# Six gate chunks of the second wide projection moved from one dense stage into three attention stages

## What is computed

```python
u = rmsnorm(x, norm_mix[l]) * (1.0 + scale1) + shift1
aq, ak, av, bq, bkv, biq, bik, biw, cq, ck, cv, g = split_cols(u @ w_in[l])
y_a = diff_attention(aq, ak, av, ...) @ w_br_a[l]
y_b = dsa_attention(bq, rmsnorm(bkv, dsa_kv_norm[l]), biq, bik, biw, ...) @ w_br_b[l]
y_c = moba_attention(cq, ck, cv, bias_c) @ w_br_c[l]
gates = jax.nn.sigmoid(g + gate_b[l]).reshape(B, S, 3, D_MODEL)
merged = gates[:, :, 0] * y_a + gates[:, :, 1] * y_b + gates[:, :, 2] * y_c
x = x + gate1 * (merged @ w_o[l])
```

## Time and profile before

| | us |
|---|---|
| median of three runs | 1955.89 |
| lowest and highest run | 1954.1, 1958.25 |
| span of the profiled execution | 1951.6 |
| PE busy in it | 1747.7 (90%) |
| DVE busy | 1018.7 (52%) |
| ACT busy | 826.7 (42%) |

### The profile page before, as it was taken

One profiled execution on the slowest core, in us unless ns is written; L12 is line 12 of the kernel. 1 busy time (PEld: TensorE's weight loads), 2 busy tenths in 40 slices (PEclk: granted clock), 3 DMA queues, 4 the chain that ended last, 5 costly groups with the idle time before them and its releaser, 6 DMA issues.

```text
span 1951.6 us, 22498 instructions
## 1 busy us (share of the span) xinstructions
PE 1747.7 (90%) x8447; PEld 1421.4 (73%) x8447; DVE 1018.7 (52%) x1239; ACT 826.7 (42%) x979; POOL 75.6 (4%) x122
## 2 busy tenths in 40 slices
PE   6999968799989999899899888999889896779996
PEld 6788857688868888798655576888677783558885
DVE  4545555454454545455666454545457653555444
ACT  4555523365543434334433333655334443314342
POOL 0000000000000000000000001000010010000000
PEclk9999989999989999999656798999989986789999
DMA  8565633566554556525344536655545520345550
GB/s 286 168 191 185 214 119 97 194 194 189 180 180 152 168 187 193 172 82 167 106 141 123 201 103 206 216 181 192 173 175 175 170 91 11 133 158 193 192 174 22
DMA packets 197807, 314.82 MB, mean 161 GB/s; under 512 B 16185, under 2 KB 120661, under 8 KB 197232
## 3 DMA queue, kind: packets, MB, share of 16 engines
q1 hardware_dynamic: 191824, 288.90, 45.1%
q0 software_dynamic: 5920, 25.06, 3.6%
HBM read 309.71 MB, written 4.21 MB: 161 GB/s over the span
## 4 chain that ended last, share of the span: by engine, by line
PE 85%; DVE 7%; ACT 2%; issue 2%; POOL 1%; PEld 1%; DVEq 1%; DMA 0%; PEldq 0%; ACTq 0%; POOLq 0%
PE ps L1865 24%; PE ps L1867 23%; PE ps L1866 23%; PE ps L2143 2%; PE ps L1911 2%; PE ps L2128 1%; DVE wlo L1218 1%; PE ps L1952 1%; PE ps L2037 1%; PE ps L2119 1%; DVE gain L1266 1%; PE ps L2139 1%; DVE xn L1288 1%; PE ps L2191 1%; ACT xn L778 1%
## 5 line engine op out<-in xcount | busy, mean ns | idle before, releaser
L1218 DVE TENSOR_TENSOR wlo<-raw,whi 128x2048 fp32r<-128x2048 f32 x255 | 579.0, 2290 | 305.1 <-ACT whi L722 304.4
L722 ACT ACTIVATE whi<-raw 128x2048 fp32r<-128x2048 f32 x255 | 481.2, 1910 | 177.6 <-PE ps L1867 163.2
L1865 PE MATMUL ps<-wlo,aT_hi 128*128 128x512 f32 (+1 forms) x1280 | 499.9, 391 | 18.9 <-issue 8.3
L1867 PE MATMUL ps<-whi,aT_hi 128*128 128x512 f32 (+1 forms) x1280 | 493.3, 385 | 0.0
L1866 PE MATMUL ps<-whi,aT_lo 128*128 128x512 f32 (+1 forms) x1280 | 493.1, 385 | 0.0
L1865 PEld LDWEIGHTS ps<-wlo,aT_hi 128*128 128x128 f32 x1280 | 243.9, 191 | 68.5 <-issue 10.5
L1867 PEld LDWEIGHTS ps<-whi,aT_hi 128*128 128x128 f32 x1280 | 243.2, 190 | 48.1
L1866 PEld LDWEIGHTS ps<-whi,aT_lo 128*128 128x128 f32 x1280 | 244.0, 191 | 45.2
L1865 PE MATMUL ps<-wlo,hT_hi 128*128 128x512 f32 x480 | 187.2, 390 | 8.4 <-DVE hT_lo L1327 6.0
L1867 PE MATMUL ps<-whi,hT_hi 128*128 128x512 f32 x480 | 187.0, 389 | 0.0
L1866 PE MATMUL ps<-whi,hT_lo 128*128 128x512 f32 x480 | 186.8, 389 | 0.0
(11 more groups left out here) (274 smaller groups left out, 1445.8 us busy)
## 6 DMA issues: line engine op xcount, KB each, us to landing
raw<-in_ffn_w_in SPq DMA_DIRECT2D x176, 512.0 KB, 4.8
raw<-in_ffn_w_out SPq DMA_DIRECT2D x88, 512.0 KB, 4.3
raw<-in_w_ff SPq DMA_DIRECT2D x64, 512.0 KB, 4.8
raw<-in_ada_w SPq DMA_DIRECT2D x48, 512.0 KB, 4.7
raw<-in_w_in SPq DMA_DIRECT2D x48, 512.0 KB, 4.6
raw<-in_xattn_w_kv SPq DMA_DIRECT2D x32, 512.0 KB, 6.7
raw<-in_xattn_w_q SPq DMA_DIRECT2D x16, 512.0 KB, 5.4
raw<-in_xattn_w_o SPq DMA_DIRECT2D x16, 512.0 KB, 6.3
```

Source lines behind the costliest of these rows:

```text
L722: act.activation(to, of, ACT.Copy).then_inc(hi_ready[slot], 1)
L1218: dve.tensor_tensor(lo, of, hi, ALU.subtract).then_inc(lo_ready[slot], 1)
L1865: pe.matmul(o, lh, rl, start=start, stop=False, skip_group_check=True)
L1867: return pe.matmul(o, lh, rh, start=False, stop=stop, skip_group_check=True)
```

## The change

Only the index chunk, `aq`, `ak` and `av` stay in `wide_inputs`. Each attention stage now runs two of the gate chunks on PE, whole, ahead of the transposes of units 0 and 4, when the scores of units 1 and 5 (2 and 6 in `moba`) are already queued. `gate_part` writes them to two PSUM banks of one half of the tokens each, and DVE's `keep_gate` adds them to the bias later. To free those banks, `diff` holds two units of scores instead of three. The splits of the gate slabs, and of the chunks that follow a stage, stand between the units in ACT's and DVE's queues. The two `dsa` stages are one of eight units. The sigmoids move to `merge`, three of 128 x 2048 in place of six of 128 x 1024. The choice of keys for tokens 128 to 255 runs all eight rounds in one piece in `wide_inputs`; that for tokens 0 to 127 is in `sparse_inputs`.

```diff
                 def wide_inputs(self):
...
-                    chunk(w, COLS["g"], 512, 0)
...
-                    for c in range(1, 6):
-                        chunk(w, COLS["g"] + 512 * c, 512, 2 * ((c + 1) % 2))
...
+                def diff(self):
+                    stages.next()
+                    self.gate(0)
+                    self.gate(1)
...
+        def gate_place(c):
+            return 2 * ((0, 1, 1, 0, 1, 0)[c]), (6, 7) if c < 4 else (3, 7)
```

PE, the new helper and its call in `diff` (`dsa` and `moba` call it with chunks 2, 3 and 4, 5):

```diff
+                def gate_part(self, c, q):
+                    (pair, banks), t, s = gate_place(c), q // 2, q % 2
+                    if c and s == 0:
+                        pe.wait_ge(gate_kept, 2 * c + t - 1)
+                    if t == 0:
+                        pe.wait_ge(lo_ready[pair + s], uses.next(pair + s))
+                    tok = slice(t * P, (t + 1) * P)
+                    for r in range(4):
+                        k = 4 * s + r
+                        last = parts(ps[:, banks[t], :], aT_hi[:, k, tok], aT_lo[:, k, tok], ...
...
-                    score(1)
                     for u in range(8):
-                        if u + 2 < 8:
-                            score(u + 2)
-                        self.turn_probs(u, u % 2, 6, depth=3, banks=1)
+                        if u + 1 < 8:
+                            score(u + 1)
+                        if u % 4 == 0:
+                            for q in range(4):
+                                self.gate_part(u // 4, q)
+                        self.turn_probs(u, u % 2, 4, depth=3, banks=1)
                         if u:
                             values(u - 1)
```

ACT in `diff` (in `dsa` and `moba` two splits stand likewise after units 0 and 1, and two after units 5, 6 or 6, 7):

```diff
                     exps(0)
-                    exps(1)
                     for u in range(8):
+                        if u + 1 < 8:
+                            exps(u + 1)
                         keep(u)
-                        if u + 2 < 8:
-                            exps(u + 2)
                         if u:
                             out(u - 1)
+                        if u < 2:
+                            split(2 + u)
+                        if u == 4:
+                            self.gate_used(0)
+                        if u > 5:
+                            split(u - 6)
```

DVE in `diff`:

```diff
                     top(0)
-                    top(1)
                     for u in range(8):
+                        if u + 1 < 8:
+                            top(u + 1)
                         weigh(u)
-                        if u + 2 < 8:
-                            top(u + 2)
+                        if u < 2:
+                            split(2 + u)
+                        if u in (2, 4):
+                            self.keep_gate(0, u // 2 - 1)
+                        if u == 6:
+                            self.keep_gate(1, 0)
+                        if u > 5:
+                            split(u - 6)
+                    self.keep_gate(1, 1)
```

More of the change, by code:

```diff
@@ L445, in skip, with gate, dsa @@
                     stages.next()
-                ada = diff_bias = diff = latent = dsa = skip
+                ada = diff_bias = latent = skip
+                def gate(self, c):
+                    chunk(A["w_in_2"][0], COLS["g"] + 512 * c, 512, gate_place(c)[0])
+                def diff(self):
+                    stages.next()
+                    self.gate(0)
+                    self.gate(1)
+                def dsa(self):
+                    stages.next()
+                    self.gate(2)
+                    self.gate(3)
                 def moba(self):
                     stages.next(2)
+                    self.gate(4)
+                    self.gate(5)
                 def wide_inputs(self):
@@ L1011, in rectify, with gate_used @@
                                     act.activation(o, o, ACT.Relu).then_inc(relu_made, 1)
-                    chunks(10, evac, transfers=[(1, 6)], after=rectify)
+                    chunks(4, evac, after=rectify)
                     leave()
+                def gate_used(self, c):
+                    for s in range(2):
+                        done.next(gate_place(c)[0] + s)
                 def keep_bias(self, b):
@@ new lines, in dsa @@
+                    exps(0)
+                    for u in range(8):
+                        if u + 1 < 8:
+                            exps(u + 1)
+                        keep(u)
+                        if u == 4:
+                            latent_out(0)
+                        if u == 5:
+                            out(0)
+                        if u < 2:
+                            split(u)
+                        if u == 4:
+                            self.gate_used(2)
+                        if u in (5, 6):
+                            split(u - 3)
@@ L1112, in dsa @@
+                    latent_out(1)
+                    out(1)
+                    self.gate_used(3)
+                    units.next(8)
+                    groups.next(2)
                     leave()
@@ new lines, in wide_inputs, with choose_keys, keep_gate @@
+                    chunks(4, evac, after=choose)
+                    leave()
+                def choose_keys(self, t):
+                    step(dve.tensor_scalar(sel[t], work[t].rearrange("p (k n) -> p k n", n=P), -2.0e38, NEG,
+                                           ALU.is_gt, ALU.mult))
+                def keep_gate(self, c, t):
+                    pair, banks = gate_place(c)
+                    if c == 0:
+                        dve.wait_ge(gate_b_in, 32)
+                    dve.wait_ge(gate_summed, 2 * c + t + 1)
+                    at = bgate[:, t, 512 * c:512 * c + 512]
+                    dve.tensor_tensor(at, at, ps[:, banks[t], :], ALU.add).then_inc(gate_kept, 1)
+                    if t:
+                        for s in range(2):
+                            done.next(pair + s)
@@ L2311, in dsa @@
                     score(0)
-                    for u in range(4):
-                        if u + 1 < 4:
+                    for u in range(8):
+                        if u + 1 < 8:
                             score(u + 1)
-                        self.turn_probs(u, t, 2 + u % 2)
-                    units.next(4)
-                    pe.wait_ge(probs_kept, units.n)
-                    for m in range(t + 1):
-                        last = pe.matmul(ps[:, 4, :], kvn[:, m, :], PTd[:, :, m, :], start=m == 0, stop=m == t)
@@ L2320, in dsa @@
[L2320 to L2326 removed]
+                        if u % 4 == 0:
+                            for q in range(4):
+                                self.gate_part(2 + u // 4, q)
@@ L2328, in moba @@
+                        self.turn_probs(u, u // 4, 2 + u % 2)
+                        if u == 4:
+                            values(0)
+                        if u == 5:
+                            expand(0)
+                    values(1)
+                    expand(1)
+                    units.next(8)
+                    groups.next(2)
                 def moba(self):
```

227 lines of the change are left out of this document (135 added, 92 removed).

## The result

The changed kernel takes 2025.9 us (median of 4 runs, 2019.3 to 2029.9), the kernel before 1956.2 beside it (1954.1 to 1958.3): a ratio of 1.035, with an interval of 1.033 to 1.037. It is slower by 3.5%. The forecast was 2024.4 us. The profiled execution of the kernel after took 2026.6 us and has a span of 2024.4.

A forecast was written before the change was run, and what follows sets the result against it. It took PE to bound `wide_inputs` and the chain from `score` to `values` the attention stages; -61.6 + 1.6 + 44.2 + 6.5 + 39.1 + 38.7 = +68.5 took the profile to 2020.1, the median to 2024.4 us, range 2010 to 2036.

The forecast's parts named there:

- The splits, the main term: Attention stages: four splits in each of three stages lie exposed on the chain, 4.3 us each, 51.6 us in all.
- `diff` step by step: `diff` walked from its first score: 66.0 us against 22.4 before, +44.2 with 0.6 for a slow chunk 0.
- Slow starts: Gate chunks: one that begins after the clock has fallen pays its first 4 us at half rate, 2.1 us more.
- a slow start for all six chunks: Gate chunks: by the skill page's rule all six would start slow, making the sum some 3.5 us higher.
- The wide stage: `wide_inputs`: six chunks leave, DVE's queue then sets the end, -61.6 us; bias transposes after it at half rate, +1.6.
- `sparse_inputs`: `sparse_inputs`: key rounds on DVE delay the splits, +4.5 us, and some 2 for falling clocks, +6.5 in all.
- `dsa`: `dsa`: two chunks, exposed splits and the rest take 66.8 us against 27.7 before, +39.1.
- `moba`: `moba`: two chunks, exposed splits and the rest take 57.2 us against 18.5 before, +38.7.
- The clock did not stay up: Rival, attention stages: gate chunks keep PE at 2.4 GHz, so the time is 2000 us; chance 0.09.
- the splits were not half hidden: Rival, attention stages: ACT reaches the splits earlier, half of 51.6 us goes, giving 1999 us; chance 0.08.
- no slab was late: Rival: a gate slab or the index pieces are waited for, 2035 us and more; chance 0.06.
- PE sets the pace: Rival, attention stages: softmax and splits run beneath the chunks, each stage lasts PE's work, 1945 us; chance 0.04.

The follow-up runs named there:

- experiment 1: The changed kernel with the four splits of each attention stage queued so they can run under its gate chunks, ACT's halves ahead of `keep`; 1964.4 us.
- experiment 3: The kernel before the change with two units of scores in flight in `diff` instead of three, nothing else; 1968.1 us.
- experiment 5: The changed kernel with a quarter of a gate chunk ahead of each unit's transpose and ACT's split halves ahead of `keep`; 1947.5 us.
- experiment 8: The kernel of experiment 6 with one key round behind each unit's `weigh` in `diff`, instead of four behind each of two units; 1934.3 us.
- experiment 6: The kernel of experiment 5 with the key choice moved as in experiment 4; 1942.8 us.
- experiment 4: The changed kernel with the key choice moved: tokens 128 to 255 into `diff`, tokens 0 to 127 under the first chunk of `sparse_inputs`; 2009.8 us.

## Why the prediction was right

**The splits, the main term.** Foreseen: 12 x 4.3 us, all on the chain. Measured: 4.14 or 4.15 us from ACT's half to DVE's next instruction in all twelve, so 49.7 us, and in experiment 1 they are gone under the chunks. The mechanism (ACT's `keep` waits for a transpose behind the whole chunk) stands in the rows around 1510.75. What hiding them gives back is 61.6, not 51.6 us; the 10 more are mostly the clock (11.5 us of busy time), which the forecast held apart from them.

**`diff` step by step.** Scores 0.9 (0.85 foreseen); chunk 0 up to the transpose 11.3 (10.9, and 0.6 allowed); transpose to DVE's next `top` 4.7 (5.05); from there to the second split 3.1 (3.4); split 4.14 (4.3); units up to the score of 5, 6.7 and that score 1.15 (8.9 together); chunk 1 with its hand-over 12.0 (12.5); transpose of 4 to the third split 8.7 (8.1); split 4.14; `weigh` and `out` 2.6 (2.8); split 4.14; the last gate half 0.8 (0.7). The sum is 64.3 against 66.6: no step is off by more than 1.1. Its difference of 3 us to the old stage outside chunks and splits came as 2, made of the 9.9 of experiment 3 less what the chunks hide.

**Slow starts.** The first matmuls of chunks 0 to 5 in the kernel after, in order of time on PE:

```profile
1499.11 0.50 PE L1962 MATMUL ps<-wlo,aT_hi 128*128 128x512 f32 x1
...
1530.13 0.79 PE L1962 MATMUL ps<-wlo,aT_hi 128*128 128x512 f32 x1
...
1611.37 0.77 PE L1962 MATMUL ps<-wlo,aT_hi 128*128 128x512 f32 x1
...
1639.88 0.99 PE L1962 MATMUL ps<-wlo,aT_hi 128*128 128x512 f32 x1
...
1676.03 3.78 PE L2344 MATMUL ps<-gain,cst 128*128 128x512 f32 x4 [0.52 <-ACTq L722]
...
1682.35 0.79 PE L1962 MATMUL ps<-wlo,aT_hi 128*128 128x512 f32 x1
...
1711.23 0.79 PE L1962 MATMUL ps<-wlo,aT_hi 128*128 128x512 f32 x1
```

From a chunk's first matmul to its 48th is 47 x 0.228 = 10.7 us at full rate. They took 10.8, 11.3, 13.2, 12.8, 12.0 and 12.9: 8.8 us over it in all, where the forecast had 7.8. Two places were missed, both at the start of `moba`. I took chunk 4 to be fast, as it follows dense `values` and transposes; but those transposes are themselves at half rate, 3.78 us where they were 1.98 before, +1.8 that the sum lacks, and chunk 4 starts slow, some 1.3 more. The last splits of `dsa` had idled PE ahead, for 5.25 and 5.06 us.
The Trainium skill, "TensorE: Matmul & The Clock Gate", section "HAM oscillation — how this bites in real kernels", describes a kernel whose every burst behind a long wait starts slow. The prediction read it as a slow start for all six chunks. The trace agrees for chunks 2 to 5, hardly for chunk 1 (0.6 us) and not for chunk 0 (0.1): the slow time behind the 5.2 us wait fell on the bias transposes ahead of chunk 0 (+1.8), and that behind the 5.0 us wait in `diff` at least in part on the units ahead of chunk 1 (the four matmuls of `values` of unit 1 take 1.06 us, those of unit 3, behind chunk 1, 0.67). The excess of 8.8 us lies nearer to the 7.8 of the forecast than to the 11.3 by that rule.

**The rest of the sum.** The wide stage was off by 0.4, its bias transposes by 0.2. `sparse_inputs` is +6.4 for +6.5, and PE's wait for the late split is the 4.5 of the working:

```profile
1589.25 0.45 PE L1962 MATMUL ps<-aT_lo,whi 128*128 128x256 f32 x1 [4.47 <-DVE wlo L1275]
```

`dsa` is 1.3 under its term and `moba` 0.3 over it, one chunk dearer and the units cheaper. PE's busy time rose by 13.8 us (under 15 foreseen); no slab was waited for. All that lies behind the first line of the table came to +67.9 against +68.5. That the median was met to 1.5 us is in part luck. The terms were off both ways (`diff` -2.3, `dsa` -1.3, the transposes of `moba` +1.8). The profile came out 4.3 us above the 2020.1 foreseen for it, with 4.9 in the unchanged code, but the median lies only 1.5 us above its span where the forecast added 4.3. And the runs of the kernel after spread over 10.5 us.

**The rivals.** The clock did not stay up (0.73), the splits were not half hidden, no slab was late. *PE sets the pace* was put at 1945 us if a split costs under 0.9 us. With the splits hidden in experiment 1 it was 1964, and 1955 with the keys moved too: hidden splits do not suffice with whole chunks, since in `diff` and `dsa` the units between two chunks have no cover. In the whole kernel it came true only with pieces cut to the unit: experiment 5 at 1947.5, and experiment 8 at 1934.3 us.

What stays open: why `dsa` remains at a clock of 0.92 to 0.93 in experiments 6 and 8 where `moba` has 1.00. In experiment 6 the clock is 0.83 over the first 9.8 us of `dsa`, 1.00 or nearly (0.93) over most of the rest, and 0.69 over its last 4.3. The first stretch follows a wait of PE of 4.2 us for DVE just ahead of the stage, the last one a wait of 1.5 us; no run removes either.

## What to carry to other kernels

Work moved onto an idle engine is worth the idle time only if what it needs from the other engines (here the splits) can run beneath it: look, for each such step, at what stands ahead of it in its queue and whether that waits for the moved work itself. Cut filler into pieces of the size of the gaps, on every engine, where the work between has little in flight: the same work took 2025.9 or 1934.3 us by the size of its pieces and their places in the queues, with 1956 to 1958 before. When a forecast removes idle time of PE, add what the clock will give back in the same stretch.

## What the runs showed of the chip

- Idle time of PE can cost more than itself. `moba`, the same 148 matmuls: 40.2 us of PE at 0.74 with the splits exposed, 32.5 at 1.00 with the splits under the chunks. The share of busy time alone does not tell the clock: `moba` before had PE busy 16.5 of 18.5 us at 0.54.
- Bias transposes of the same form, four of 128x512, take 1.95 to 1.98 or 3.75 to 3.78 us. Those of `diff` took 3.75 where PE had waited 5.2 us just ahead of them (after, experiments 1 and 5) and 1.95 where it had waited 0.9 (before, experiments 4 and 6). Behind short waits the waits do not settle it: those of `moba` took 3.78 us in experiment 5 and 1.98 in experiment 6, behind the same `dsa` code (39.0 and 39.1 us) and the same waits of 1.5, 0.5, 0.7 and 0.5 us. No run shows what does.
- The spread of the runs depends on how many there are: the kernel before spread over 4.2 us in 4 runs and over 9.9 in the 11 beside experiment 8, so the 10.5 us in 4 runs of the kernel after are no sure sign that it varies more.
- The start of `wide_inputs` moved by 5.9 us between ten profiles with the same work up to there, one of each kernel; whether from program to program or from execution to execution is not shown.
